# Adaptive-norm weight sums on GpSimd instead of TensorE, in a two-part block kernel on one Trainium2 core

## The reference

```
cond = jax.nn.silu(c)                              # 1 x 1024
mod = cond @ w_ada[l] + b_ada[l]                   # 1 x 6144
sh_m, sc_m, g_m, sh_f, sc_f, g_f = jnp.split(mod[:, None, :], 6, axis=-1)
h = _rms(x, norm_mix[l]) * (1.0 + sc_m) + sh_m
proj = h @ w_in[l]
... attention and state-space mixer give y_attn and y_ssd ...
x = x + g_m * (mixed @ w_out[l])
h = _rms(x, norm_ffn[l]) * (1.0 + sc_f) + sh_f
x = x + g_f * _moe(h, w_router[l], b_router[l], w_gu[l], b_gu[l], w_dn[l], b_dn[l])
```

## Time and profile before

| | before |
|---|---|
| median of three runs | 2022.99 us |
| profiled execution: its time | 2021.93 us |
| its span in the profile | 2020.1 us |
| PE busy | 1944.1 us (96%) |
| DVE busy | 658.2 us (33%) |
| ACT busy | 406.6 us (20%) |
| POOL busy | 65.0 us (3%) |
| read from HBM | 580.13 MB |

### The profile page before, as it was taken

One profiled execution on the slowest core, in us unless ns is written; L12 is line 12 of the kernel. 1 busy time (PEld: TensorE's weight loads), 2 busy tenths in 40 slices (PEclk: granted clock), 3 DMA queues, 4 the chain that ended last, 5 costly groups with the idle time before them and its releaser, 6 DMA issues.

```text
span 2020.1 us, 22280 instructions
## 1 busy us (share of the span) xinstructions
PE 1944.1 (96%) x8948; PEld 1107.0 (55%) x8948; DVE 658.2 (33%) x1358; ACT 406.6 (20%) x861; POOL 65.0 (3%) x93
## 2 busy tenths in 40 slices
PE   7999999999989999999989999999999999999998
PEld 3767886333333333333333333766888456778863
DVE  1487513122122122121212222552333435433353
ACT  2134213111110111111101112253211033422110
POOL 0000000000000000000000000110011011001100
PEclk9999999999999999999999999999999999999999
DMA  9754358999999999999999999263543434335440
GB/s 374 271 211 185 133 213 338 417 432 431 431 434 430 433 431 431 434 430 433 431 431 434 430 428 413 74 231 104 168 151 141 167 114 169 123 125 167 139 171 24
DMA packets 93287, 582.19 MB, mean 288 GB/s; under 512 B 4312, under 2 KB 49504, under 8 KB 75680
## 3 DMA queue, kind: packets, MB, share of 16 engines
q1 hardware_dynamic: 91552, 574.65, 70.2%
q0 software_dynamic: 1664, 6.56, 1.0%
HBM read 580.13 MB, written 2.63 MB: 288 GB/s over the span
## 4 chain that ended last, share of the span: by engine, by line
PE 75%; DMA 20%; DVE 3%; ACT 1%; issue 0%; SPq 0%; DVEq 0%; ACTq 0%
PE psum L385 51%; PE psum L730 11%; DMA ring<-w_gu 9%; PE psum L663 9%; DMA work<-w_gu 9%; DMA ring<-w_dn 2%; PE psum L2270 1%; DVE work L1911 1%; PE psum L717 1%; PE psum L701 1%; DMA ring<-w_ada_first 1%; PE psum L1128 0%; PE psum L1170 0%; PE psum L1159 0%; PE psum L619 0%
## 5 line engine op out<-in xcount | busy, mean ns | idle before, releaser
L385 PE MATMUL psum<-normed,ring 128*128 128x256 f32 (+1 forms) x2400 | 498.8, 369 | 0.1
L385 PEld LDWEIGHTS psum<-normed,ring 128*128 128x128 f32 x2400 | 435.6, 191 | 59.2 <-issue 4.4
L663 PE MATMUL psum<-work,normed 128*64 128x512 f32 x1024 | 233.1, 609 | 25.4 <-DMA work<-w_gu 25.4
L663 PE MATMUL psum<-ring,normed 128*64 128x512 f32 x1024 | 234.8, 613 | 23.0 <-DMA ring<-w_gu 22.4
L385 PE MATMUL psum<-work 128*128 128x128 f32 (+7 forms) x1216 | 222.5, 353 | 0.2 <-ACT work L1492 0.2
L385 PE MATMUL psum<-ring,work 128*128 128x512 f32 (+1 forms) x464 | 197.5, 578 | 0.1
L385 PEld LDWEIGHTS psum<-work 128*128 128x128 f32 (+2 forms) x1216 | 147.7, 185 | 84.5 <-issue 73.5
L663 PEld LDWEIGHTS psum<-work,normed 128*64 128x64 f32 x1024 | 77.7, 140 | 178.7 <-issue 176.6
L663 PEld LDWEIGHTS psum<-ring,normed 128*64 128x64 f32 x1024 | 75.3, 141 | 179.6 <-issue 160.9
L385 PE MATMUL psum<-ring,normed 128*128 128x512 f32 (+1 forms) x368 | 152.1, 567 | 0.7 <-PE psum L385 0.4
L385 PEld LDWEIGHTS psum<-ring,work 128*128 128x128 f32 x464 | 87.4, 190 | 100.0 <-issue 98.7
(11 more groups left out here) (339 smaller groups left out, 1377.3 us busy)
## 6 DMA issues: line engine op xcount, KB each, us to landing
work<-w_gu SPq DMA_DIRECT2D x31, 4096.0 KB, 29.8
ring<-w_gu SPq DMA_DIRECT2D x29, 4096.0 KB, 30.0
work<-w_dn SPq DMA_DIRECT2D x15, 4096.0 KB, 30.1
ring<-w_dn SPq DMA_DIRECT2D x14, 4096.0 KB, 30.1
ring<-w_in SPq DMA_DIRECT2D x23, 2048.0 KB, 9.2
ring<-w_up SPq DMA_DIRECT2D x44, 1024.0 KB, 7.1
ring<-w_down SPq DMA_DIRECT2D x10, 2048.0 KB, 7.8
ring<-w_ada SPq DMA_DIRECT2D x8, 2048.0 KB, 8.9
```

Source lines behind the costliest of these rows:

```text
L385: return pe.matmul(out, lhsT, rhs, start=first, stop=last, **kw)
L663: ins = pe.matmul(b[r], self.hgT[:, 2 * q + k, r], w[:, 2 * k + e, n0:n0 + 512], start=q == 0 and k == 0, stop=q == QUARTERS - 1 and k == ...
```

## The change

Blocks 4 to 11 no longer go through PE and ACT. GpSimd loads them itself, through its own queue, in halves of 1 MB into slot 3 of the ring, which nothing else uses in the front from then on. It multiplies each of the eight tiles of 128 x 512 by its column of `cond` (in place) and adds it to a running sum. When a half has been added up, the same half of the next block is loaded. The order is 6, 7, 4, 5, 8, 9, 10, 11. The sum over partitions stays on PE, in other places of its list: `mod_rows(4)` and `(5)` go from the start of the front to its attention output, `sum_mod(8)` and `(9)` to the state-space output, `mod_rows(10)` and `(11)` into the routing. The sums lie in `acc`, in `gain` (4 and 5, which start from the bias in one partition) and in the experts' output buffer (10 and 11, which is free only from `yx` on).

All other weights of the front now use slots 0 to 2 by a table (`places`). The half of `gu 0` that lies in slot 3 waits for all eight sums, the other half for the last `wso`. Block 1 of `w_ada` comes as two transfers of 1 MB and its first two products wait only for the first.

```diff
 def front_slots():
+    return {("ada", 0): 2, ("ada", 1): 0, ("top",): 1, ("ada", 2): 3, ("ada", 3): 2, ("bottom",): 0,
+            ("win", 2): 1, ("win", 3): 2, ("wkv",): 0, ("win", 4): 1, ("win", 5): 2,
+            ("win", 6): 0, ("gate", 0): 1, ("win", 7): 2, ("gate", 1): 0, ("gate", 2): 1, ("gate", 3): 2,
+            ("wo",): 0, ("wso", 0): 1, ("wso", 1): 2, ("wout", 0): 0, ("wout", 1): 1}
+ADA_SLOT = 3
+ADA_ORDER = (6, 7, 4, 5, 8, 9, 10, 11)
...
+    def load_first(self, sp, io, S, used, part):
+        name, cols = ("gu", 0, 0), slice(part * SLOT, (part + 1) * SLOT)
+        sp.wait_ge(*used)
+        sp.dma_start(self.mem.place(S.no(name))[:, cols], self.source(io, name, 0)[:, cols])\
+          .then_inc(*((self.second_in[0], 16) if part else S.fills(*name)))
...
+                if j == 1:
+                    sp.dma_start(slot(S.no(name), 1, 2048)[:, 0], io["w_ada_first"][j][:, 0:2048]).then_inc(tables_in, 16)
+                    wait_free(name)
+                    sp.dma_start(slot(S.no(name), 2, 2048)[:, 1], io["w_ada_first"][j][:, 2048:]).then_inc(*S.fills(*name))
...
-        X.load_when_free(sp, io, SP, PAIR_SLOTS[0], [slot_used(("wso", j)) for j in range(2)])
+        X.load_first(sp, io, SP, (acc_ready, len(ADA_ORDER)), 1)
+        X.load_first(sp, io, SP, slot_used(("wso", 1)), 0)
         sp.wait_ge(mixed_ready, 4)
-        for j in range(2):
-            sp.wait_ge(*B.released("m", 10 + j))
+        sp.wait_ge(*B.ready("m", 9))
...
     def gpsimd(pool):
+        step(pool.memset(gain, 0.0))
+        def load_half(n, half):
+            src = io["w_ada"][ADA_ORDER[n] - 4][:, 2048 * half:2048 * half + 2048]
+            pool.dma_start(ada_w[:, half].rearrange("p k n -> p (k n)"), src).then_inc(ada_half[half], 16)
+        def sum_columns(j, between=None):
+            n, out = ADA_ORDER.index(j), ada_sum(j)
+            started = j in (4, 5)
+            for half in range(2):
+                pool.wait_ge(ada_half[half], 16 * (n + 1))
+                for i in range(4):
+                    k = 4 * half + i
+                    w = ada_w[:, half, i]
+                    step(pool.tensor_scalar(w if k or started else out, w, cond[:, k, 0:1], None, ALU.mult))
+                    if k or started:
+                        step(pool.tensor_tensor(out, out, w, ALU.add))
+                    if k == 3 and between:
+                        between()
+                if n + 1 < len(ADA_ORDER):
+                    load_half(n + 1, half)
+            pool.nop().then_inc(acc_ready, 1)
...
+        sum_columns(6)
+        pool.wait_ge(line_ready, 1)
         pool.dma_start(line_one.rearrange("a (h n) -> (a h) n", h=HEADS), line_sb).then_inc(line_out, 16)
+        sum_columns(7, spread_lines)
+        pool.wait_ge(gain_in, 16)
+        sum_columns(4, bias_table)
+        sum_columns(5)
+        sum_columns(8)
+        pool.wait_ge(*B.ready("m", 6))
+        sum_columns(9)
+        pool.wait_ge(*B.ready("yx", 1))
+        sum_columns(10)
+        sum_columns(11)
...
         def mod_rows(j):
-            pe.wait_ge(ada_in, j - 1)
+            pe.wait_ge(acc_ready, ADA_ORDER.index(j) + 1)
             pe.wait_ge(*B.empty("m", j))
-            matmul(pe, bank("m", j), ones, acc[:, j % 3]).then_inc(*B.fills("m", j))
+            matmul(pe, bank("m", j), ones, ada_sum(j)).then_inc(*B.fills("m", j))
...
         conv_inputs(0)
-        ada(4)
...
         transposes(("kiT",), [ki2[:, t] for t in range(NT)])
-        mod_rows(4)
...
         x1_transposes(1, 2)
+        mod_rows(10)
         router(1, range(6, KC))
+        mod_rows(11)
         pe.wait_ge(rows_in, 1)
...
     def scalar(act):
-            ada_rows(acc[:, j % 3], j)
...
+        for half in range(2):
+            take(late_rows[:, half], bank("m", 10 + half), "m", 10 + half)
         act.wait_ge(route_ready, 1)
```

More of the change, by code:

```diff
@@ L135, with __init__ @@
 class Uses:
-    def __init__(self, full, free, names, inc=1, base=None, twice=(), first=0):
+    def __init__(self, full, free, names, inc=1, base=None, twice=(), first=0, places=None):
         n = len(full)
@@ L216, in front_banks @@
[L216 to L219, removed]
+    u += [("yi", 0, g) for g in range(SG)] + [("row", 1, j) for j in range(4)]
+    u += [("yx", g) for g in range(SG)] + [("ga", 4), ("ga", 5), ("brow",)] + [("yi", 1, g) for g in range(SG)]
@@ L874, in first_block @@
     mixed_ready, x1_ready = sem("mixed_ready"), sem("x1_ready")
-    route_ready, route_exp, mask_ready, gates_ready = (sem(n) for n in ("route_ready", "route_exp", "mask_ready", "gates_ready"))
+    route_ready, route_exp, mask_ready = (sem(n) for n in ("route_ready", "route_exp", "mask_ready"))
+    acc_ready, ada_half = sem("acc_ready"), [sem("ada_half" + str(half)) for half in range(2)]
     X = Experts(mem, sem, "")
@@ L949, in sync @@
         sp.dma_start(x, io["x"].rearrange("(t p) d -> p t d", p=P)).then_inc(x_in, 16)
-        order = front_slots()
+        held = {}
         def slot_used(name):
@@ L963, in slot_used, with wait_free @@
                              "wout": ("x1", 1, 2 * j) if kind == "wout" else None}[kind])
+        def wait_free(name):
+            earlier = held.get(S.no(name))
+            if earlier is not None:
+                sp.wait_ge(*slot_used(earlier))
+            held[S.no(name)] = name
         def load(src, *name):
-            if order.index(name) >= SLOTS:
-                sp.wait_ge(*slot_used(order[order.index(name) - SLOTS]))
+            wait_free(name)
             n = src.shape[-1]
@@ L1385, in tensor @@
         y_transposes(0)
-        mod_rows(10)
+        mod_rows(5)
         attn_out((2,))
-        ada(11)
         y_transposes(1)
         attn_out((3,))
-        mod_rows(11)
         pe.wait_ge(*B.released("yT", 1, 1))
-        for j in range(2):
-            w = wait_slot("wso", j)
-            by_feature(("ys", 2 * j), w, 0, yT)
-            by_feature(("ys", 2 * j + 1), w, 256, yT)
+        w = wait_slot("wso", 0)
+        by_feature(("ys", 0), w, 0, yT)
+        sum_mod(8)
+        by_feature(("ys", 1), w, 256, yT)
+        w = wait_slot("wso", 1)
+        by_feature(("ys", 2), w, 0, yT)
+        sum_mod(9)
+        by_feature(("ys", 3), w, 256, yT)
         w = [wait_slot("wout", j) for j in range(2)]
@@ L1985, in vector @@
             signal(TT(m, m, two(v), ALU.add), mixed_ready, p + 1)
+        take_rows(4, 0)
+        gate_attention(0)
+        gate_attention(1)
+        take_rows(5, 1)
+        gate_attention(2)
+        gate_attention(3)
+        gate_state(0)
+        take_mod(8)
+        gate_state(1)
+        gate_state(2)
+        take_mod(9)
+        scale_columns(a2, prm("norm_ffn"), 32)
+        signal(TT(w_r, w_r, rows(a2, E), ALU.mult), router_ready, 1)
+        gate_state(3)
         def residual(t, j):
```

155 lines of the change are left out of this document (66 added, 89 removed).

## The result

| | before | after |
|---|---|---|
| median, us (6 runs each) | 2021.5 | 2032.7 |
| lowest to highest | 2019.6 to 2023.9 | 2030.0 to 2037.6 |
| profiled execution, us | 2021.9 | 2037.6 |
| its span, mean granted clock | 2020.1, 0.989 | 2035.8, 0.981 |

The ratio is 1.0059, its 95% interval 1.0044 to 1.0075. I had forecast 2013.5 and a gain; it is a loss of 11 us.

What follows compares the result with a forecast made beforehand. The experts go at the pace of the weight stream, whose start the front sets: PE, then DVE, then PE. Terms -2.7 - 0.55 - 7.4 + 1.2 = -9.5 us gave 2012.4, as a median 2013.5; range 2009 to 2046.

Steps and rivals of the forecast that it cites:

- what the sum leaves out: DVE's stretch: DVE keeps its durations while GpSimd works beside it; price taken as nothing, upper end 53 us.
- the sum: Whole kernel: the gains and losses in the front added up, -9.5 us, giving 2013.5; chance 0.43 for 2011 to 2016.
- The first rival: 128 to 179 us: GpSimd holds up 42 two-input DVE steps, costing 27 to 53 us; chance 0.29.
- DVE's stretch: Front, 127.9 to 178.8 us, where the chain runs over DVE; one softmax step leaves it, gaining 0.55 us.
- GpSimd's durations: Block sums on GpSimd: add 1.34 us, multiplication at most as long, 23 us a block, all hidden.
- rival 2: Bias table issued late by slower GpSimd blocks, up to +11 us; 0.12 near its end, shared with the first rival nearly cancelled.
- rival 4: End of GpSimd's sums: SP waits with gu 0, 1 us for each beyond 278; small, contained in rival 2.
- PE before DVE's stretch: Front before about 128 us: block 4 and its row sum leave PE, so DVE's scoring starts 2.7 us earlier.
- PE behind it: Front after DVE's stretch, from 182.3 us: blocks 8 to 11 leave PE, gaining 7.4 us.
- slack of 0.7 us at the second chunk's product: Near 234.83 us: margin left for DVE to follow the faster PE; where gone, up to a microsecond.
- Routing: Routing: two new row sums on PE delay the router by 0.35 and first gather by 0.87, +1.2 us.
- Edits at nothing: Block 1 in two transfers, fewer ACT copies, three ring slots: no cost; 1 to 3 us if second w_out misses.

Runs made afterwards that it cites:

- Experiment 1: The changed kernel, but GpSimd sums blocks 6 and 7, issues the bias table, then rests until DVE's last convolution; 2031.6 us against 2020.5 before, ratio 1.0044.
- x_pause: The kernel of Experiment 1: the changed kernel with GpSimd resting until DVE's last convolution; 2031.6 us, ratio 1.0044 to before.
- x_both: The changed kernel with blocks 6, 7, 8 back on PE; GpSimd sums 4, 5, rests, then 9 to 11; 2014.9 us against 2020.4 before, ratio 0.9968.
- x_busy: The changed kernel plus unused PE products, ten ahead of the first logits, twelve for the wait ahead of x's transposes (they ran behind it); 2050.6 us.
- experiment 2: The kernel before with only block 1 of w_ada in two 1 MB transfers; 2020.5 us against 2020.5, ratio 1.0001.
- x_fill2: The changed kernel plus ten unused PE products inside PE's wait ahead of x's transposes; 2035.8 us, ratio 1.0080 to before.

## Why the prediction was wrong

- **The failed step** is in "what the sum leaves out": that DVE keeps its durations while GpSimd works beside it. I took nothing, by one overlap of 0.14 us, and the text itself said that it proves little. It was the tail of an addition, and in after an addition lets a step go some 0.2 us before its end. What the runs showed in its place: a step that meets an addition waits for nearly all that is left of it. Convolution: 36 x 0.283 = 10.2 us; its 12 multiplications 2.5; the long softmax step at 176.73 1.1. That is 13.8 of the 14 us of the stretch. Experiment 1 gives all of it back: the stretch is 50.4 us there (125.54 to 175.96), against 50.9 in before and 65.0 in after.
- **The first rival's size.** It said 42 steps and 27 to 53 us. Of the convolution's steps one in three was held for 0.9 us, the others ran free, since GpSimd, held by DVE in turn, fell into step: a channel took 3.1 us, the time of one multiplication and one addition. I left out the steps with one input, which are held too, and gave the scoring half a sentence: it lost 8.3 us, as DVE's stretch began 5.6 late instead of 2.7 early. 14 + 8.3 = 22, under the 27.
- **GpSimd's durations.** The multiplication takes 1.56 us unhindered and 1.74 on average, not "at most as long as the add". A block takes 24 to 28 us instead of 23. The bias table was issued at 114.34 instead of 108; no wait of DVE for it is in the trace, as DVE was late itself. The last sum ended at 284.5 instead of 272, but SP asked for it at 305. So neither rival 2 nor rival 4 happened.
- **PE before DVE's stretch**, 2.7 us: 2.3 of it reached DVE's stretch in x_pause, which began it at 125.54 instead of 127.86, and 1.35 in x_both, 126.51. In both GpSimd still summed beside the first scoring steps (511 and 586 ns instead of 418).
- **PE behind it**, 7.4 us: right with the clock whole. From the group of 32 of the earlier trace rows at 182.28 to x1's transposes before took 321.87 - 182.28 = 139.6 us, x_busy 130.4; the blocks are 7.4 of these 9.2, and a fall of the clock to 0.83 at 190 to 200 us that before has accounts for 1.7. In after the same way took 138.3, so all but 1.3 us of the gain was gone. So a second thing failed, which the sum took for granted: that PE's work keeps its durations. I did not ask what idle time of PE's would bring. Nor did the slack of 0.7 us at the second chunk's product last: PE waited there, 0.26 us in after and 1.1 in x_pause.
- **Routing**, +1.2 us: +1.0 up to the first gather (14.9 us from x1's transposes instead of 13.9). At the second gather the term is 0, by the clock: before's first gather took 3.06 us, with the clock at 0.83 at 330 to 340 us, and after's 2.04.
- **Edits at nothing**: right as far as tested. Block 1 in two transfers is nothing (experiment 2), and x_both shows that three slots for the other weights, and the row sums in the routing, leave room for a gain of 5.5 us.
- **What else**: x_both's best execution is 9.5 us under before, as much as the sum. That is agreement in size and not a check of its terms: in its profile the clock and the late blocks cost several microseconds, and there is no profile of a best one.

## What to carry to other kernels

Before giving idle GpSimd anything to do, look at what DVE does in the same microseconds, and whether DVE is on the path there: where GpSimd added without rest, each DVE step of 0.485 us with two inputs in SBUF took 1.39. Work that PE can do beside a stretch that DVE sets belongs there, but only as much as PE finishes with DVE: in x_both two blocks ran over and cost 2.8 us. GpSimd's hours are those in which DVE is idle. And a pause needs a place for the work that it displaces: count the blocks against the last date at which each is wanted.

## What the runs showed of the hardware that I had not expected

- GpSimd's multiplication of 128x512 by a column takes 1.56 us, more than its addition of two tensors, 1.27 us. The Trainium skill's page "GPSIMD Engine Reference", section "4.1 Engine selection", calls one-input work there roughly line-rate; the measurement decides.
- GpSimd's clearing, with no input at all, makes a DVE multiplication by a column take 724 ns instead of 413, and leaves a DVE step with two inputs at 485.
- Beside additions of 128x512 one after another every such step takes 1.39 us, beside multiplications one in three or so is held, by 0.3 to 0.4 us.
- The hold goes both ways: 3.48 us for a GpSimd multiplication that met a DVE step of 3.34 us.
- After a wait of 13 us PE's clock was at 0.50, and in both profiles of after it fell a second time some 50 us later, at 250 us, in a stretch where PE was idle for 0.26 us; that fall costs 5.0 us (89.8 against 84.9 from there on), the one in the wait 1 to 3 us behind the wait (131.7 in x_fill2 and 138.3 - 5.0 in after, against 130.4), and the second is likely what divides the runs of one kernel into two groups. Idle time is not what every fall follows: in x_both the clock fell twice between 210 and 240 us with PE busy.
